# A decoder step whose first norm is folded into its transposes, whose FFN norm is applied after the product, and whose transposed keys are copied page by page

## Time and profile before

| | |
|---|---|
| time of 3 runs, median (lowest to highest) | 2252.89 us (2250.77 to 2255.76) |
| the profiled execution's own time | 2252.39 us |
| its span, first to last instruction | 2250.8 us |
| mean granted TensorE clock | 0.963 |
| busy: TensorE / weight loads / VectorE / ScalarE / GpSimd | 94% / 89% / 54% / 35% / 3% |

### The profile page before, as it was taken

How to read it: one execution, slowest core, us unless ns; L and a number is a source line. 1 busy time by engine, 2 the same in 40 slices (tenths; PEclk the granted TensorE clock), 3 DMA queues, 4 the chain that set the end, 5 groups by cost and what they waited for, 6 DMA issues and landing times.

```text
span 2250.8 us, 40554 instructions
## 1 busy us (share of the span) xinstructions
PE 2122.3 (94%) x16438; PEld 2001.4 (89%) x16438; DVE 1206.2 (54%) x1424; ACT 797.4 (35%) x1010; POOL 63.5 (3%) x85
## 2 busy tenths in 40 slices
PE   4999998999899999999999787999999999999997
PEld 3999897899677878999998666999999999999997
DVE  3354565343555646667455446666654466566444
ACT  3333342243333333333344323333333333333333
POOL 0001011111000000000000000000000000000000
PEclk8899997999999999999999988999999999999998
DMA  7146434445588687556444351545445554554553
GB/s 247 38 150 189 131 98 157 132 152 175 169 287 309 242 307 272 158 174 216 167 141 159 131 187 59 165 154 181 149 141 173 172 182 154 164 172 138 173 159 114
DMA packets 305493, 384.82 MB, mean 171 GB/s; under 512 B 6146, under 2 KB 278690, under 8 KB 304626
## 3 DMA queue, kind: packets, MB, share of 16 engines
q1 hardware_dynamic: 300530, 365.72, 49.4%
q0 software_dynamic: 4896, 18.13, 2.5%
HBM read 370.94 MB, written 12.88 MB: 171 GB/s over the span
## 4 chain that ended last, share of the span: by engine, by line
PE 89%; DVE 5%; ACT 2%; issue 1%; SPq 1%; DMA 1%; POOL 0%; PEldq 0%; DVEq 0%; PEld 0%; ACTq 0%; POOLq 0%
PE bank L1713 19%; PE bank L1714 19%; PE bank L1717 18%; PE bank L1727 8%; PE bank L1731 6%; PE bank L2174 4%; PE bank L2173 4%; PE bank L2178 4%; PE bank L1724 1%; PE bank L1953 1%; PE bank L1952 1%; PE bank L1956 1%; DVE w_lo L1051 1%; DVE n_tmp L1083 1%; ACT w_hi L639 1%
## 5 line engine op out<-in xcount | busy, mean ns | idle before, releaser
L1051 DVE TENSOR_TENSOR w_lo<-raw,w_hi 128x2048 fp32r<-128x2048 f32 (+2 forms) x289 | 604.8, 2096 | 584.5 <-ACT w_hi L639 580.1
L1713 PE MATMUL bank<-xn_hi,w_hi 128*128 128x288 f32 x3152 | 875.0, 304 | 45.0 <-DVE xn_lo L1091 26.0
L1714 PE MATMUL bank<-xn_lo,w_hi 128*128 128x288 f32 x3152 | 867.0, 301 | 0.0
L639 ACT ACTIVATE w_hi<-raw 128x2048 fp32r<-128x2048 f32 (+2 forms) x289 | 504.2, 1746 | 687.3 <-PE bank L1717 471.8
L1713 PEld LDWEIGHTS bank<-xn_hi,w_hi 128*128 128x128 f32 x3152 | 608.4, 193 | 58.3 <-issue 41.6
L1714 PEld LDWEIGHTS bank<-xn_lo,w_hi 128*128 128x128 f32 x3152 | 608.3, 193 | 0.1
L1717 PE MATMUL bank<-xn_hi,w_lo 128*128 128x288 f32 x3152 | 450.7, 295 | 0.0
L1717 PEld LDWEIGHTS bank<-xn_hi,w_lo 128*128 128x128 f32 x3152 | 430.1, 189 | 0.0
L2173 PE MATMUL bank<-f_hi,w_hi 128*128 128x288 f32 x704 | 191.4, 296 | 0.0
L2174 PE MATMUL bank<-f_lo,w_hi 128*128 128x288 f32 x704 | 190.8, 297 | 0.0
L2173 PEld LDWEIGHTS bank<-f_hi,w_hi 128*128 128x128 f32 x704 | 132.5, 188 | 0.1
(11 more groups left out here) (363 smaller groups left out, 1764.6 us busy)
## 6 DMA issues: line engine op xcount, KB each, us to landing
raw<-w_in_dram SPq DMA_DIRECT2D x44, 2048.0 KB, 8.6
raw<-w_ffn_gate_dram SPq DMA_DIRECT2D x22, 2048.0 KB, 8.0
raw<-w_ffn_up_dram SPq DMA_DIRECT2D x22, 2048.0 KB, 8.0
raw<-w_ffn_down_dram SPq DMA_DIRECT2D x32, 1408.0 KB, 6.4
raw<-cache_k_dram SPq DMA_DIRECT2D x64, 512.0 KB, 5.3
raw<-cache_v_dram SPq DMA_DIRECT2D x64, 512.0 KB, 5.2
raw<-w_out_dram SPq DMA_DIRECT2D x8, 2048.0 KB, 8.1
w_pm_raw<-w_proj_m_dram SPq DMA_DIRECT2D x8, 1024.0 KB, 5.1
```

The lines of the kernel that those rows point to most:

```text
L639: nc.scalar.activation(like(wh[ph.half(c)], src), src, ACT.Copy).then_inc(hi_ready, 1)
L1051: nc.vector.tensor_tensor(like(wl[ph.half(c)], src), src, like(wh[ph.half(c)], src).bitcast(F32), ALU.subtract).then_inc(slot_read[ph.slot ...
L1713: mm(out, wh[half][:, k, :], rh[:, k, 0:n], start=k == 0, stop=False)
L1714: mm(out, wh[half][:, k, :], rl[:, k, 0:n], start=False, stop=False)
```

## The change

It has four parts.

**The start.** `x` goes to tiles of its own, so that raw slots 0 and 1 are free for the first weights at once; `p_in` is gone. SP's order is first half of `x_prompt`, constants, second half, `x_sample`, gate weights, first weights. The 13 small loads are issued by ScalarE. The squares of a token are added along its row (ScalarE twice, VectorE once, each 2048 columns with an accumulator). The factor of each token is put on a diagonal matrix `xdiag`, and TensorE multiplies the rows of `x` by it, which transposes and scales at once; ScalarE and VectorE round and split that with the gain straight from PSUM, while TensorE does the gate tile five feature groups behind. The raw transposes of `x` (still needed for the residual) and the chain of gate steps are spread over the first pass of `p_ml`, at fixed places between its tiles (`first_step`, `x_tiles`, `x_copy`).

**The FFN's norm.** The up tiles take `x * gain` without the factor; each quarter of the 16 feature groups is rounded and split as soon as `p_xo` has added it (`xg_hi`, `xg_lo`). GpSimd adds up the squares in 31 steps; one matmul with ones behind the first up tile makes the mean, and the factor `fr` is multiplied in where the gate is evacuated (`up_scale`, now VectorE) and once more after the sigmoid (in `up_sig`). ScalarE's copy of the gate is gone, its Exp reads the scaled gate.

**The keys of a page.** The score loop steps over whole pages: eight transposes, then eight score products of the page before. ScalarE copies both halves of an even page (banks 2 and 3), VectorE both of an odd one (banks 4 and 5, into new tiles `KTb2`). VectorE takes in the rows of the batch before ahead of the copies, and TensorE waits for that before page 1.

**Bookkeeping.** Three semaphores of the last norm become one, unused ones are dropped, and indices are renumbered.

```diff
-    p_in = Phase(plan, 1, [(2, 1), (1, 1)], 0, 0)
...
+        KTb2 = [at(f"d_KT2{n}", [P, 4, P], dp_at + n * 4 * 4 * P) for n in range(2)]
...
         def _(sp):
-            sp.dma_start(blob[:], a["blob"]).then_inc(const_in, 16)
+            xp = a["x_prompt"].rearrange("b (t p) d -> (b t) p d", p=P)
+            for t in range(2):
+                sp.dma_start(xrow0[:, t, :], xp[t]).then_inc(x_in[t], 16)
+                if not t:
+                    sp.dma_start(blob[:], a["blob"]).then_inc(const_in, 16)
+            sp.dma_start(xrow1[:], a["x_sample"].rearrange("b t d -> (b t) d")).then_inc(x_in[2], 16)
...
         def _(gp):
...
+            pc = Chain(gp, pch)
+            for m in range(KT):
+                gp.wait_ge(c_xo, m + 1)
+                pc.run(nc.gpsimd.tensor_tensor(fsq[:, m % 2, :] if m else fsum[:], xT[:, m, :], xT[:, m, :], ALU.mult))
+                if m:
+                    pc.sync()
+                    pc.run(nc.gpsimd.tensor_tensor(fsum[:], fsum[:], fsq[:, m % 2, :], ALU.add))
+            gp.wait_ge(pch, 2 * KT - 1)
+            nc.gpsimd.engine_nop().then_inc(sq_ready, 1)
...
         def _(act):
...
+            for n, name in enumerate(("norm_mix", "norm_xattn", "norm_mem", "norm_ffn")):
+                act.dma_start(grow[16 * n:16 * n + 16, :], a[name].rearrange("l (k p) -> (l k) p", p=P)).then_inc(params_in, 16)
...
+            act.wait_ge(x0_step, 1)
+            act.wait_ge(x_in[0], 16)
+            nc.scalar.activation(xsq[0][:], xrow0[:, 0, :], ACT.Square, accum_out=xss[:, 0:1]).then_inc(x0_step, 1)
+            act.wait_ge(x_in[2], 16)
+            nc.scalar.activation(xsq[2][0:NS], xrow1[:], ACT.Square, accum_out=xss[0:NS, 2:3]).then_inc(x0_step, 1)
+            act.wait_ge(x0_step, 1 + x0_ms)
+            nc.scalar.activation(xu[:], xms[:], ACT.Ln).then_inc(x0_step, 1)
+            act.wait_ge(x0_step, 1 + x0_ln)
+            nc.scalar.activation(xr[:], xu[:], ACT.Exp, scale=-0.5).then_inc(x0_step, 1)
+            hi(p_gate, 0, 0, 0, gate_src)
+            act.wait_ge(gains_set, 2)
+            for k in range(KT):
+                act.wait_ge(x0_mm, k + 1)
+                nc.scalar.activation(xh[:, k, :], B[2 + k % 6][:, 0:NT], ACT.Copy, scale=gains[:, k:k + 1]).then_inc(x0_hi, 1)
...
+                for n in range(0, PAGES, 2):
+                    for q in range(2):
+                        act.wait_ge(d_tr, b * 16 + (2 * n + 1 + q))
+                        if not q:
+                            act.wait_ge(d_ss, b * PAGES + (n + 1))
+                        last = a_copy(KTb[q][:], B[2 + q][:].rearrange("p (h c) -> p h c", c=P))
+                    last.then_inc(d_kta, 1)
...
+            def xg_hi(c):
+                for k in range(4 * c, 4 * c + 4):
+                    act.wait_ge(c_xo, k + 1)
+                    nc.scalar.activation(xh[:, k, :], xT[:, k, :], ACT.Copy, scale=gains[:, 48 + k:49 + k]).then_inc(nh_ready, 1)
+            for j in range(5):
+                if j < 4:
+                    hi(p_xo, 0, j // 2, j, xo_src(j))
+                else:
+                    hi(p_up[0], 0, 0, 0, src256(p_up[0].slot(0), 0))
+                if j >= 2:
+                    xg_hi(j - 2)
+            xg_hi(3)
...
         def _(dve):
...
+            for k in range(KT):
+                dve.wait_ge(x0_mm, k + 1)
+                dve.wait_ge(x0_hi, k + 1)
+                nc.vector.scalar_tensor_tensor(xl[:, k, :], B[2 + k % 6][:, 0:NT], gains[:, k:k + 1], xh[:, k, :].bitcast(F32),
+                                               ALU.mult, ALU.subtract).then_inc(x0_lo, 1)
+                if k == 7:
+                    lo(p_gate, 0, 0, 0, gate_src)
...
+            def xg_lo(c):
+                for k in range(4 * c, 4 * c + 4):
+                    dve.wait_ge(c_xo, k + 1)
+                    dve.wait_ge(nh_ready, 4 * 2 + k + 1)
+                    last = nc.vector.scalar_tensor_tensor(xl[:, k, :], xT[:, k, :], gains[:, 48 + k:49 + k], xh[:, k, :].bitcast(F32),
+                                                          ALU.mult, ALU.subtract)
+                last.then_inc(xn_ready, 1)
...
+            def up_scale(f, i, t):
+                dve.wait_ge(gemm_done, p_up[f].conv(i, t + 1))
+                nc.vector.tensor_tensor(fg[:, t, :], G[p_up[f].bank(t)][:, 0:NT], fr[:], ALU.mult).then_inc(f_g, 1)
+                nc.vector.engine_nop().then_inc(evac_done[p_up[f].bank(t)], 1)
...
         def _(pe):
...
+            for k in range(KT):
+                out = B[2 + k % 6]
+                if k >= 6:
+                    pe.wait_ge(x0_lo, k - 5)
+                for t in range(2):
+                    one(out[:, t * P:(t + 1) * P], xrow0[:, t, k * P:(k + 1) * P], xdiag[:, t, :])
+                one(out[:, TP:NT], xrow1[:, k * P:(k + 1) * P], xdiag[0:NS, 2, 0:NS]).then_inc(x0_mm, 1)
+                if k >= 5:
+                    gate_k(k - 5)
...
                     if gemm:
                         tile(p_ml, i, j // 2, j, j)
+                    if gemm and not attn:
+                        first_step(j)
...
-                for n in range(17):
...
+                for n in range(PAGES + 1):
+                    if n == 1:
+                        pe.wait_ge(d_h, b + 1)
+                    if n < PAGES:
+                        if n % 2 == 0:
+                            pe.wait_ge(kv_landed[n // 2], b * 64 + 32)
+                        for h in range(H):
+                            c = n % 2 * H * DH + h * DH
+                            last = tr(B[2 + 2 * (n % 2) + h // 4][:, h % 4 * P:(h % 4 + 1) * P], ring(n // 2)[:, c:c + DH])
+                            if h % 4 == 3:
+                                last.then_inc(d_tr, 1)
                     if n:
+                        page, kt = n - 1, (KTb, KTb2)[(n - 1) % 2]
+                        pe.wait_ge((d_kta, d_ktd)[page % 2], b * (PAGES // 2) + (page // 2 + 1))
+                        for h in range(H):
+                            m = h % GROUPS
                             last = one(B[6 + page // 4][m * NS:(m + 1) * NS, (page % 4) * P:(page % 4 + 1) * P],
+                                       qpad[:, h * NS:(h + 1) * NS], kt[h // 4][:, m, :], start=h < GROUPS, stop=h >= GROUPS)
...
-            pe.wait_ge(c_xo, 4)
-            norm(3, NT)
+            pe.wait_ge(c_xo, 12)
             for f in range(2):
...
+                    if not j and not f:
+                        pe.wait_ge(sq_ready, KT // 2 * 2 + 1)
+                        mm(B[2][:, 0:NT], ones[:], fsum[:], start=True, stop=True).then_inc(sq_used, 1)
```

More of the change, by code:

```diff
@@ L238, in build @@
         top[0] = free0
-        first_scratch = norm_scratch(0, ("sq", "tmp", "ms", "r", "u"))
+        xrow0 = put("x_p_rows", [P, 2, D])
+        xdiag = put("x_diag", [P, 3, P])
+        xss, xms, xr, xu = [put(f"x_{n}", [P, 3]) for n in ("ss", "ms", "r", "u_")]
+        assert top[0] <= ha0
+        xrow1 = at("x_s_rows", [NS, D], xT_at)
+        xsq = [at(f"x_sq{t}", [P, D], xn_at + t * 4 * D) for t in range(3)]
         top[0] = ha0
@@ L341, in build @@
         fg, fe, fa = [put(f"f_{n}", [P, 2, NT]) for n in ("g", "e", "a")]
+        fr, fms, fu, fsum = [put(f"f_{n}", [P, NT]) for n in ("r", "ms", "u", "sum")]
+        fsq = put("f_sq", [P, 2, NT])
         assert top[0] <= nc.sbuf_usable_end
@@ L994, in up_body @@
                 for j in range(4):
-                    if j or f or not first:
+                    if j > 1 or f or not first:
                         hi(p_up[f], i, j // 2, j, src256(p_up[f].slot(j // 2), j % 2))
@@ L1610, in up_body @@
                         up_mul(f, i - 1, j)
-                    if j or not first:
+                    if j >= 2:
+                        up_scale(f, i, j - 2)
+                    if not first or j > (0 if f else 1):
                         lo(p_up[f], i, j // 2, j, src256(p_up[f].slot(j // 2), j % 2))
@@ new lines, in gate_k @@
+            def gate_k(k):
+                half, out = p_gate.half(0), G[p_gate.bank(0)][:, 0:NT]
+                pe.wait_ge(x0_lo, k + 1)
+                if k == 0:
+                    pe.wait_ge(hi_ready, 1)
+                mm(out, wh[half][:, k, :], xh[:, k, :], start=k == 0, stop=False)
+                mm(out, wh[half][:, k, :], xl[:, k, :], start=False, stop=False)
+            for k in range(KT):
[7 more added lines that the diff above has]
+                    gate_k(k - 5)
@@ new lines, in _, with x_tiles @@
+            for k in range(KT - 5, KT):
+                gate_k(k)
+            pe.wait_ge(slot_read[2], 1)
+            for k in range(KT):
+                last = mm(G[p_gate.bank(0)][:, 0:NT], wl[p_gate.half(0)][:, k, :], xh[:, k, :], start=False, stop=k == KT - 1)
+            last.then_inc(gemm_done, 1)
+            def x_tiles(s):
+                if s >= 3:
+                    pe.wait_ge((tp_even, tp_odd)[(s - 3) % 2], (s - 3) // 2 + 1)
+                if s:
+                    t, k4 = (s - 1) // 4, (s - 1) % 4
```

397 lines of the change are left out of this document (211 added, 186 removed).

## The result

The changed kernel takes **2216.5 us** in the median of four executions (2207.8 to 2222.7), against 2251.8 before: a ratio of 0.984, 95% interval 0.980 to 0.988. That is 35 us less where 56 were predicted, half a us beyond the upper end of the range. The profiled execution took 2207.8, the shortest of the four; why executions of one program differ by 15 us is part of the answer.

The account below looks back on a forecast made before the run. The prediction took TensorE, busy for 94% of the span, to bound the kernel. Start 25, FFN's norm 17 and score loop 14 sum to 56 us; 2252.4 - 56 = 2196 us, range 2180 to 2216.

Parts of the forecast that it names:

- The loop: Start, loop over k: four k at half clock, 12 more at 0.87, last pairs 1.3, `w_lo` 2.1; together 19 us.
- Rival 2: Start is late: small loads behind the weights (9 us) or half clock through the loop (10.4 us); 2206, chance 0.13.
- the lower of the two cases: Start: small loads overtake the weights, land before 21.2 and cost nothing; the upper, about 30, costs 9 us.
- 6 more if the clock never falls: Start, upper bound: 6 us beyond its gain of 25 if TensorE's clock never falls.
- Rival 1: FFN's norm: GpSimd works beside VectorE without exclusion, ends near 1363, 28 us won; 2185, chance 0.2.
- rival 4: Up passes: VectorE becomes their bound and the kernel is slower; 2271 at 29 us a pass; chance 0.03.
- 0.22: Score loop: us left of a 0.94 us half page for two changes between transposes and scores.
- Rival 3: Score loop: the change saves nothing, as the gap follows the groups, not the change of kind; 2210, chance 0.12.

Follow-up runs that it names:

- 68 + 14 kernel: Changed kernel plus 68 and 14 extra fp32 products of 128 columns on TensorE while it waits ahead of the loop over k; 2198.0 us, ratio 0.977.
- halves-by-engine kernel: Changed kernel with each whole page of transposed keys copied half by ScalarE and half by VectorE; 2210.6 us, ratio 0.980.

## Why the prediction was wrong

**The step that failed** is "The loop", in the start: "that is four k; 12 more at 0.87". It took the length of the half-clock stretch from a tile behind a pause, 5.2 us, and carried it over to this loop. Here the stretch lasts 16 to 36 us, in one profile the whole loop. The trace of the kernel before could have said so: its granted clock is at half from 24.2 to 34.4, from 44.6 to 61.7 (all but the end of the gate tile) and from 65.1 to 75.3, and the 5.2 us are only the end of the last. Two of its windows, as the earlier trace rows:

```profile
50.00:60.00 10.00, 8.42 (x32) 7.73 (x33) 7.30 (x11) 2.33 (x2) 0.00 (x0) 0.50 0.01 2
...
70.00:75.00 5.00, 4.73 (x20) 4.73 (x21) 4.71 (x3) 0.00 (x0) 0.00 (x0) 0.50 0.00 2
```

The 0.77 of the earlier trace rows also reads as full what lies ahead of that trace's first record of the clock, at 17.3. Term by term, up to the second p_ml pass:

| term | predicted | measured |
|---|---|---|
| loop over k begins | 21.2 | 22.5 |
| the loop at full clock, without `w_lo` | 15.2 (16 x 0.87 + 1.3) | 20.2 (23.39 to 43.55 in the 68 + 14 kernel) |
| what half clock adds to it | 1.7 | 8.9 in the profile (29.1 - 20.2), 15.3 where it lasted longest (35.5 - 20.2) |
| `w_lo` products | 2.1 | 2.1 |
| first p_ml pass | 59.4 | 58.3 |
| second pass begins | 99.6 | 112.1; mean of nine 114.4 |

The 15.2 of the second line counts five of the 16 gate pairs twice (each k with one, and five more), 1.3 us too much, which hides a part of that line's error. The second error of the start is that the sum ended at the second pass. It took the passes behind the start as the same whatever came before; they are 5 us longer in the mean of the profiles, the stages behind the scores 3.5, and in the time of the whole nothing measurable is left of the start's 25 us. Rival 2 had the mechanism, a clock at half through the loop, with 10.4 us and a chance of 0.13 shared with the small loads; it was not likely enough and lacked the p_ml passes.

**The other steps of the start.** The 1.3 us of the first line are mostly `x_sample`, which landed at 15.8 and not at 14.9, and 0.2 us on VectorE, where the mean of squares waits behind the copies of the gains; the prediction asked only whether the small loads come before the diagonal, not what is queued behind the wait for them. They land at 18.0, so the lower of the two cases held. The last was issued at 8.46, 5 us behind the gate's weights, and landed ahead of these (3.11 + 17.4 = 20.5). So they did overtake them. That agrees with the rings of their own and the turns between them that the Trainium skill gives the two engines (DMA: Bandwidth & Descriptors, section Queues, rings and completion order). The narrow products cost 0.33 a pair at full clock, 44.44 to 44.77, as much as three wide ones of 0.11, where half of a wide one's price was put in; the gate pair costs 0.37 and not 0.27. Five k at 0.98 in place of 0.6 and eleven at 1.24 in place of 0.87 make 6.0 us, the 5 of the second line and most of the 1.3 that the double count hid. The bound "6 more if the clock never falls" has no working: the sum itself put 1.7 on half clock.

**The FFN's norm** was right in mechanism and near in size: 17 predicted, 19 to 20 measured; the second up tile 16.9 us behind p_xo's end where the sum had 19.5. The exclusion is shown: with one GpSimd operation in place of 31, splits fall from 0.94 to 0.46; without nearly all of GpSimd's work 8.4 us are won. Rival 1 is out (its 1363 did not follow from its own terms, 1339.7 + 18.6 = 1358.3). The Trainium skill's rule on the shared port (SBUF — State Buffer, section Who interferes with whom) agrees with a GpSimd operation that takes 2.73 beside a `lo` of 2.75 and 0.67 alone. The sum had added 0.6 and 0.51 in turn; both are longer (0.88 and 0.94, the one inside the other), but GpSimd had started on earlier chunks while p_xo still ran.

**The up passes** take 281.00 us without a pause, VectorE 195.4 of them (196 predicted): rival 4 is out.

**The score loop** gave 18 to 20.5 in place of 14. Its term "0.22" for the changes was too low: the rows have 0.20 and 0.17 at each pair, 0.37, and the score products' loads take 0.38 and not 0.56. So a page falls from 1.885 to 1.60, 18 us over 64; the rest comes at the ends of the batches. Rival 3 is out, and the halves-by-engine kernel shows that no copy sets the period.

**In sum** 0 + 20 + 18 = 38 in place of 25 + 17 + 14; 35 were measured. Had the clock been at full level in the loop, the kernel would have come out at 2198, by the 68 + 14 kernel, and the forecast of 2196 would have been right in part by luck: 5 us of product cost and 1.3 at the diagonal against 7 more from FFN and scores.

**What stays open.** Why the half-clock stretch ends at 38.8 in one execution and 58.1 in another of the same instructions; why the extra products were at full clock behind 5.8 us and the loop's products not within 16; why the p_ml passes fall to half for longer behind some starts, and why the stages behind the scores take 3.5 us more behind the changed one; and whether 8 products ahead of the loop are enough.

## What to carry to other kernels

Work that is moved into the first microseconds of a kernel runs at the clock that it finds there: price it by rows at half level for its whole length, or keep TensorE at work while it waits for its first data, here on products of 128 columns, sized to end before the data comes. A gain ahead of stages whose length varies by the clock has to be looked for at the end of the kernel, in several executions, since the profiled one can be the shortest.

## What the runs showed of the hardware

- TensorE's clock stayed at half level through 16 to 36 us of the loop's products (PE busy throughout, its weight loads for 17.87 of 20.98 us), in one profile with 3.8 us of work ahead of them too. With 82 extra products ahead it was at full level from 7.0 us, 5.8 us behind the first of them, and from the loop's first product.
- The granted clock in the windows reads 1.00 where the trace has no record yet (until 43.1 in the changed kernel); the durations there (1.04 against 0.61 for the same four products) say half.
- The p_ml passes' length, 322 to 337 us for the same instructions, goes with their granted clock, 0.91 to 0.86; the longest stretch at half, 17.1 to 34.1 us, is in the last mLSTM.
- A pair of records of 32 rows and 32 columns takes 0.33 us at full clock, as much as three wide records of 128.
- VectorE's split with two inputs from SBUF takes 0.46 alone and 0.94 in turns with GpSimd; GpSimd's operation of 288 columns 0.67 and 0.88, and 2.73 if it falls behind a `lo`.
